# Paired heads in the neighbourhood attention, modulation's last third in the second block, and filter spectra from even and odd taps

## The reference

```python
# first block
s = einsum('bhqd,bhkd->bhqk', q, k) + c_i[..., :, None] - c[..., None, :]   # causal
x = layer_norm(alpha * x + concat(o_fox, o_hgrn) @ w_o)
x = layer_norm(alpha * x + (gelu(a) * u) @ w_down)          # a, u = split(conv(x @ w_up))
# second block
mod = silu(c) @ w_ada + b_ada                                # six vectors of 1024
sh1, sc1, g1, sh2, sc2, g2 = split(mod)
mod_c = silu(c_ctx) @ w_ada + b_ada
h = rmsnorm(x) * (1 + sc1) + sh1
s_nb  = einsum('brqhd,brikhd->bhrqik', rope(q), rope(k) in a window of 8x16) * scale + bias
s_ctx = einsum('brqhd,bchd->bhrqc', q, k_ctx) * scale        # 256 context tokens
p = softmax(concat(s_nb, s_ctx)); y_na = p @ concat(v, v_ctx)
K = rfft(concat(h_fwd, 0, h_bwd[:0:-1]), n=1024)             # filters, per order and channel
z = gate * irfft(rfft(z, n=1024) * K)                        # twice
x = x + g1 * gated_merge(...)                                # sh2, sc2, g2 modulate the FFN
```

## Time and profile before

| | us |
|---|---|
| median of 3 runs | 1770.71 (1770.68 to 1770.86) |
| the profiled execution | 1770.02 |
| its span, first to last instruction | 1768.2 |
| PE busy | 1663.8 (94%) |
| DVE busy | 891.2 (50%) |
| ACT busy | 657.0 (37%) |
| POOL busy | 267.3 (15%) |
| mean granted PE clock | 0.971 |

### The profile page before, as it was taken

The page is one execution under the profiler, slowest core; times in us unless marked ns, Lnnn a source line. Parts: engine busy times, 40 slices in busy tenths (PEclk is TensorE's granted clock), DMA queues, the critical chain, the costliest instruction groups (busy, mean ns, idle before and its releaser), DMA issues. The chain is left out here.

```text
span 1768.2 us, 19372 instructions
## 1 busy us (share of the span) xinstructions
PE 1663.8 (94%) x7952; PEld 1348.7 (76%) x7952; DVE 891.2 (50%) x1245; ACT 657.0 (37%) x888; POOL 267.3 (15%) x256
## 2 busy tenths in 40 slices
PE   5899989998998989999989999999799999999997
PEld 5668867767877868788788877777687888887885
DVE  6575446447787667633652543336864422223234
ACT  5544245443532233322542333333443522222222
POOL 0024302110511101100034011112432000000002
PEclk8999999999998989999999999999999999999998
DMA  7232222252244445422323322222444222222221
GB/s 276 96 131 84 72 83 91 82 197 96 84 178 167 191 167 191 145 94 95 110 90 109 119 100 87 82 75 90 175 147 167 95 93 90 89 91 92 96 72 48
DMA packets 47059, 204.86 MB, mean 116 GB/s; under 512 B 14353, under 2 KB 14737, under 8 KB 28219
## 3 DMA queue, kind: packets, MB, share of 16 engines
q1 hardware_dynamic: 37346, 172.89, 27.0%
q0 software_dynamic: 9088, 30.38, 4.9%
q10 hardware_dynamic: 536, 0.35, 0.1%
HBM read 182.60 MB, written 21.00 MB: 115 GB/s over the span
## 5 line engine op out<-in xcount | busy, mean ns | idle before, releaser
L438 PE MATMUL ps<-xh,whi 128*128 128x512 f32 (+1 forms) x1160 | 450.6, 388 | 16.4 <-DVE wlo L1563 10.4
L439 PE MATMUL ps<-xl,whi 128*128 128x512 f32 (+1 forms) x1160 | 445.0, 384 | 0.0
L440 PE MATMUL ps<-xh,wlo 128*128 128x512 f32 (+1 forms) x1160 | 442.6, 382 | 0.0
L1563 DVE TENSOR_TENSOR wlo<-raw,whi 128x2048 fp32r<-128x2048 f32 x114 | 273.7, 2401 | 277.3 <-ACT whi L1008 277.2
L1008 ACT ACTIVATE whi<-raw 128x2048 fp32r<-128x2048 f32 x114 | 217.2, 1906 | 186.8 <-PE ps L440 142.9
L438 PEld LDWEIGHTS ps<-xh,whi 128*128 128x128 f32 x1160 | 220.9, 190 | 80.6 <-issue 23.0
L440 PEld LDWEIGHTS ps<-xh,wlo 128*128 128x128 f32 x1160 | 220.4, 190 | 46.0
L439 PEld LDWEIGHTS ps<-xl,whi 128*128 128x128 f32 x1160 | 221.0, 190 | 42.3
L438 PE MATMUL ps<-whi,ah 128*128 128x512 f32 x352 | 139.7, 397 | 4.6 <-DVE al L1568 4.6
L439 PE MATMUL ps<-wlo,ah 128*128 128x512 f32 x352 | 139.5, 396 | 0.0
L440 PE MATMUL ps<-whi,al 128*128 128x512 f32 x352 | 139.5, 396 | 0.0
(11 more groups left out here) (383 smaller groups left out, 2660.6 us busy)
## 6 DMA issues: line engine op xcount, KB each, us to landing
raw<-in_w_in SPq DMA_DIRECT2D x35, 1024.0 KB, 4.9
raw<-in_ffn_w SPq DMA_DIRECT2D x33, 1024.0 KB, 4.8
raw<-in_ada SPq DMA_DIRECT2D x24, 1024.0 KB, 4.8
raw<-in_w_up SPq DMA_DIRECT2D x22, 1024.0 KB, 4.8
raw<-in_w_down SPq DMA_DIRECT2D x11, 1024.0 KB, 4.8
xd<-X POOLq DMA_DIRECT2D x8, 512.0 KB, 5.9
td<-vr POOLq DMA_DIRECT2D x16, 256.0 KB, 3.6
raw<-td SPq DMA_DIRECT2D x4, 1024.0 KB, 6.0
```

The lines of the kernel that those rows point to most:

```text
L438: pe.e.matmul(o, lh, rh, start=start, stop=False)
L439: pe.e.matmul(o, lh, rl, start=False, stop=False)
L440: return pe.e.matmul(o, ll, rh, start=False, stop=stop)
L1563: up(ve.e.tensor_tensor(lo, raw[conv_at[j] % 3][:, :], hi.bitcast(F32), ALU.subtract), "wlo")
```

## The change

Three parts, in one file.

- **Spectra.** Taps are ordered even first, then odd. One tile `dftf` holds cosines and sines for 256 frequencies. A part (`spectrum_part`) is one pair of even or odd taps' products: 32 parts of 3 matmuls where 32 halves had 6. ACT copies the even part to `spe`, the odd ones to `spo`. POOL adds and subtracts the two (16 operations on 128x512), which gives frequency f and frequency 512-f, waits for its own additions and starts the DMAs in pairs. The inverse tables of the later stage are reordered on the host.
- **Neighbourhood attention.** Items alternate between heads 2j and 2j+1. PE takes two banks every second iteration and issues four score products in a row: neighbourhood of the even head, of the odd one, context of the even head, of the odd one. POOL's biases come in the new order.
- **Modulation.** Group 2 (tiles 16 to 23) moves from FFN-up to the second block: DVE adds four tiles between the keys' and queries' rotations and four behind the conversions of the values' tiles; PE's call stands in the Hyena projection, in a row buffer of its own (`row3`). In FFN-up the tiles of groups 0 and 1 are spread over slots 1 to 19, and PE's calls stand behind slots 11 and 20; the context's channels behind slot 13. POOL's gate rows and three waits move with them.

```diff
-THIRDS = (8, 12, 20)
-def ada_beside(j):
-    return (j - 1,) if 1 <= j <= 8 else (2 * j - 10, 2 * j - 9) if 9 <= j <= 12 else (j + 3,) if 13 <= j <= 20 else ()
+ADA_UP = (1, 2, 3, 5, 6, 7, 9, 10, *range(12, 20))
+ADA_IN2 = (1, 2, 3, 4, 5, 5, 6, 6)
+def item(i):
+    return 2 * (i // 8) + i % 2, i % 8 // 2
+def bias_no(hd, v):
+    return 6 * (hd // 2) + 2 * v + hd % 2
...
-    several("dftf", 2)
+    several("dftf", 1)
...
-            def spectrum_half(n):
-                m = n // 2
-                i, f, hf = m // 4, m % 4, n % 2
-                th, tl = weights(J_DFT + i % 2)
+            def spectrum_part(n):
+                m, t = n // 2, n % 4
+                i, f = n // 8, n // 4 % 2
+                th, tl = weights(J_DFT)
                 h, l = weights(J_TAP + i)
...
-                for t in (2 * hf, 2 * hf + 1):
-                    x, c = 512 * t + P * f, slice(512 * t, 512 * t + 512)
-                    o = mm3(b[:, :], th[:, x:x + P], tl[:, x:x + P], h[:, c], l[:, c], t == 0, t == 3)
+                x, c = 1024 * (i % 2) + 256 * t + P * f, slice(512 * t, 512 * t + 512)
+                o = mm3(fills.bank["spec", m][:, :], th[:, x:x + P], tl[:, x:x + P], h[:, c], l[:, c], n % 2 == 0, n % 2 == 1)
...
-                    if 2 * j2 + part in THIRDS:
-                        ada(8 + 8 * THIRDS.index(2 * j2 + part))
-                if j2 == 5:
+                    if 2 * j2 + part in (11, 20):
+                        ada((11, 20).index(2 * j2 + part))
+                if j2 == 6:
...
                 used(J_H2 + c)
+                if c == 1:
+                    ada(2)
...
                 if i < 32:
-                    hd, t = divmod(i, 4)
-                    ht, po_ = hd // 2, 64 * (hd % 2)
-                    b = take(("as", 32 + i), "at_s", 32 + i + 1)
...
+                    if i % 2 == 0:
+                        ht, t = i // 8, item(i)[1]
+                        bs = [take(("as", 32 + i + o), "at_s", 32 + i + o + 1) for o in range(2)]
+                        for o, b in enumerate(bs):
+                            r = slice(64 * o, 64 * o + 64)
+                            keys = kr2[r, ht, :].rearrange("p (r c) -> p r c", c=64)[:, :, KC0[t]:KC0[t] + 32]
+                            pe.e.matmul(b[:, 0:256].rearrange("p (r c) -> p r c", c=32), qt[r, ht, P * t:P * t + P],
+                                        keys, start=True, stop=True)
+                        for o, b in enumerate(bs):
+                            r = slice(64 * o, 64 * o + 64)
+                            done(pe.e.matmul(b[:, 256:512], qn[r, ht, P * t:P * t + P], kc[r, ht, :],
+                                             start=True, stop=True), ("as", 32 + i + o))
                     gate_half(i)
...
-            high(J_DFT + 1)
...
-                ac.wait_ge(sig[f"kd{m % 3}"], 16 * (m // 3))
-                act(spk[m % 3][:, :], b[:, :], ACT.Copy, "sp_k", scale=2.0 / 1024)
+                u = m // 2
+                if m % 2:
+                    ac.wait_ge(sig[f"kd{u % 2}"], 32 * (u // 2))
+                    act(spo[u % 2][:, :], b[:, :], ACT.Copy, "sp_k")
+                else:
+                    ac.wait_ge(sig["kpm"], 2 * u)
+                    act(spe[:, :], b[:, :], ACT.Copy, "sp_k")
...
-            low_parts(J_DFT + 1)
+            low_parts(J_DFT)
...
                     low_parts(J_UP + 2 * j2 + part + 1)
-                    for n in (24,) if 2 * j2 + part == 21 else ada_beside(2 * j2 + part):
-                        ada(n)
+                    if 2 * j2 + part in ADA_UP:
+                        ada(ADA_UP.index(2 * j2 + part))
+                    if 2 * j2 + part in (12, 21):
+                        ada_sums((12, 21).index(2 * j2 + part))
...
                 up(ve.e.tensor_tensor(x[:, :], x[:, :], rope[:, 1, :], ALU.mult), "rt_m")
+                if n % 2:
+                    ada(16 + n // 2)
+            low_parts(J_V2 + 1)
+            ada(20)
+            ada(21)
             low_parts(J_V2 + 2)
+            ada(22)
+            ada(23)
...
                 low_parts(J_H2 + c + 1)
+                if c == 3:
+                    ada_sums(2)
...
+            ve.wait_ge(sig["gated"], 32)
...
-            def spectrum(m):
-                po.wait_ge(sig["sp_k"], m + 1)
-                po.e.dma_start(kd[m // 8, m % 8], spk[m % 3][:, :]).then_inc(sig[f"kd{m % 3}"], 16)
+            def spectrum(u):
+                i, f = u // 2, u % 2
+                a, b, s = spe[:, :], spo[u % 2][:, :], sps[u % 2][:, :]
+                po.wait_ge(sig["sp_k"], 2 * u + 2)
+                po.wait_ge(sig[f"kd{u % 2}"], 32 * (u // 2))
+                add(s, a, b, ALU.add, "kpm")
+                add(b, *((b, a) if i % 2 else (a, b)), ALU.subtract, "kpm")
+                po.wait_ge(sig["kpm"], 2 * u + 2)
+                po.e.dma_start(kd[i // 2, 4 * (i % 2) + f], s).then_inc(sig[f"kd{u % 2}"], 16)
+                po.e.dma_start(kd[i // 2, 4 * (i % 2) + 2 + f], b).then_inc(sig[f"kd{u % 2}"], 16)
...
-            spectrum(1)
             for k in range(4):
                 po.wait_ge(sig["hn_x"], k + 1)
                 c = slice(P * k, P * k + P)
                 add(orr[:, :, c], orr[:, :, c], gr[:, :, c], ALU.mult, "rec")
```

More of the change, by code:

```diff
@@ L90 @@
 rt_m hp hz mg_m gr_m f_a xa
-xg xb hd_p hx_p rec act rt_p rt_q zero bias hsum mg_a gr_x
-raw0 raw1 raw2 x0 x1d x2 x3 xsp consts mlp_in taps_in tri rows brow ncb0 ncb1 kd0 kd1 kd2 td0 td1 td2 td3 lvm ncd gated ctx tables
+xg xb kpm hd_p hx_p rec act rt_p rt_q zero bias hsum mg_a gr_x
+raw0 raw1 raw2 x0 x1d x2 x3 xsp consts mlp_in taps_in tri rows brow ncb0 ncb1 kd0 kd1 td0 td1 td2 td3 lvm ncd gated ctx tables
 tb0 tb1 tb2 tb3 rel0 rel1 vt kk0 kk1 kk2 tq0 tq1 tq2 tq3 tq4 tq5 tq6 hdl0 hdl1 hdl2 hdl3 put
@@ L157, in weight_plan @@
         plan.append(("w", ins["w_up"][i]))
-        for n in ada_beside(i - 1):
-            plan.append(("ada", ins["ada"][n]))
+        if i - 1 in ADA_UP:
+            plan.append(("ada", ins["ada"][ADA_UP.index(i - 1)]))
     several("w_down", 11)
-    several("w_in2", 20)
+    for i in range(20):
+        plan.append(("w", ins["w_in2"][i]))
+        for k, at in enumerate(ADA_IN2):
+            if i == at:
+                plan.append(("ada", ins["ada"][16 + k]))
     several("dfts", 2)
@@ L312, in build @@
         mx = [sb("mx", [P, S], F32, fs) for _ in range(2)]
-        spk = [sb("spk", [P, S], F32, fs) for _ in range(3)]
+        spe = sb("spe", [P, S], F32, fs)
+        spo, sps = ([sb(n, [P, S], F32, fs) for _ in range(2)] for n in ("spo", "sps"))
         fs.close()
@@ L870, in tensor_program @@
                 if i >= 3:
-                    hd, t = divmod(i - 3, 4)
+                    hd, t = item(i - 3)
                     c = slice(P * (hd // 2), P * (hd // 2) + P)
@@ L1301, in one @@
                     if inst == 0 and k == 3:
-                        ac.wait_ge(sig["gated"], 32)
+                        ac.wait_ge(sig["gated"], 16)
                     if k >= 4:
@@ L1416, in gate_rows @@
                 act(tm[k % 4][:, :], b[:, :], ACT.Copy, "sg")
+            tile(("adr", 2, 1))
             for i in range(34):
@@ L1712, in ada_sums @@
                 ve.wait_ge(sig["brow"], 16 * g)
+                r = row2 if g == 1 else row3
                 for h in range(2):
@@ L2351, in gpsimd_program @@
                 fox_bias(hd)
-                spectrum(2 * hd - 4)
-                spectrum(2 * hd - 3)
-            for m in range(12, 16):
-                spectrum(m)
+                spectrum(hd - 2)
+            spectrum(6)
+            spectrum(7)
             po.wait_ge(sig["pe"], at["w", J_TAP + 3])
@@ L2375, in gpsimd_program @@
                     gate_bias(0)
[L2376 to L2380 removed]
+            gate_rows(0)
+            po.wait_ge(sig["pe"], at["adr", 1, 1])
             po.e.dma_start(bcg[:, :], rows_of(ins["rows"], 4)).then_inc(sig["rows"], 16)
@@ L2428, in gpsimd_program @@
                 po.e.memset(x[:, 256:512], 0.0).then_inc(sig["zero"], 1)
-            for v in range(3):
-                bias(0, v)
-            for hd in range(8):
-                if hd < 7:
-                    bias(hd + 1, 0)
-                gate_out(2 * hd)
-                if hd < 7:
-                    bias(hd + 1, 1)
-                    bias(hd + 1, 2)
-                gate_out(2 * hd + 1)
+            for k in range(3):
+                bias(k)
+            for k in range(16):
+                n = 6 * (k // 4) + (3, 5, 6, 8)[k % 4]
+                for x in (n, n + 1) if k % 2 == 0 else (n,):
+                    if x < 24:
+                        bias(x)
+                gate_out(k)
             for n in range(2):
@@ L2537, in sync_program @@
             sp.wait_ge(sig["pe"], at["w", J_WO + 1])
-            for r, n in enumerate((6, 5, 5)):
-                sp.wait_ge(sig[f"kd{r}"], 16 * n)
+            for r in range(2):
+                sp.wait_ge(sig[f"kd{r}"], 128)
```

93 lines of the change are left out of this document (42 added, 51 removed).

## The result

The changed kernel takes 1726.6 us (median of 4 runs, 1725.28 to 1730.4) where the kernel before takes 1770.78 (4 runs). The ratio is 0.9754, with a 95% interval of 0.9737 to 0.9771: faster by 44 us, 41 to 47. The profiled execution took 1725.4 us with a span of 1723.6.

A forecast was written before the change was run, and what follows sets the result against it. The prediction took PE, busy 94% of the span, as the bound. Spectra 18.3, heads in pairs 16.7 and modulation 13.7 sum to 48.7 us; 1770.0 - 48.7 + 0.7 = 1722.0 us, range 1709 to 1733, to 1742 with rivals except the slow one.

The forecast's parts named there:

- The step ahead of the attention: Before the Fox attention: less ACT copying shortens a PE wait by 1.7 us and slow clock by 1.5, together 3.2.
- The failed term: Fox attention: 22.4 us of matmuls removed, of which 15.1 us would remain as gain after allowances for waits and POOL.
- the place at items 9 to 11: Fox loop: PE overtakes the softmax where DVE has an extra low part queued; 1.25 us subtracted.
- the rival "slower": Fox loop: small PE waits each iteration lower its clock, making the kernel slower, at worst about 1802 us; chance 0.025.
- the rival "filler hidden": Fox loop: softmax chain latency sets the pace, so parts 4 to 27 yield some 3 us; 1732 us, chance 0.11.
- two halves: Fox attention, POOL's additions: 1.0 us for delaying gating products and transposes, 1.0 us for slowing DVE's work.
- The four changes of 0.1 us: Neighbourhood attention: switching between kinds of matmul costs 0.4 us an iteration; pairing saves 0.4 a pair, 6.4 us in all.
- five slots: Neighbourhood attention: eight score passes, started in order on different rows, overlap into five slots, saving 10.3 us.
- two banks are taken at once, hence nothing: Neighbourhood attention: PE takes two banks an iteration earlier, but all have an iteration's slack; no cost.
- The first rival: Neighbourhood attention: the two heads' passes don't overlap, only fewer matmul changes gain, 6.4 rather than 16.7 us; 1732 us, chance 0.31.
- All three waits: FFN-up: PE waits of 1.64, 3.80 and 5.83 us go as modulation is spread thinner and calls stand later; 11.3 us.
- The cost at the queries: Second block: a modulation operation delays the queries' low part by 3.4 us, plus 0.9 for half clock; 4.3 us lost.

The follow-up runs named there:

- 9.9 alone: The kernel before with only the hunks of the spectra part: 1761.39 us, ratio 0.9944.
- 19.5 alone: The kernel before with only the hunks of the neighbourhood attention part: 1752.54 us, ratio 0.9890.
- on the same rows: The kernel before, with PE issuing the four score products of two successive items of one head in a row, all on the same 64 rows: 1765.86 us, ratio 0.9968.
- head by head: The changed kernel with a pair's score products reordered: neighbourhood and context of the even head, then of the odd one: 1727.76 us, ratio 0.9752.
- 20.4 alone: The kernel before with only the hunks of the modulation part: 1751.23 us, ratio 0.9885.
- mended: The changed kernel with DVE making the low part of the queries' first tile before adding modulation tile 16, later pairs likewise: 1727.01 us, ratio 0.9747.

## Why the prediction was right, and where it wasn't

The forecast was 1722.0, the result 1726.6, and the range held it. That the total came so near is in part luck. Alone, the spectra brought 8.4 us less than forecast and the two other parts 2.8 and 6.7 more, which nearly cancels; together the parts brought some 6 us less than their sum, of which the forecast knew nothing.

**Spectra: 18.3 forecast, 9.9 alone.** The step ahead of the attention was right: 3.2 forecast, and from the recurrence's earlier wait to its last one (at 225.59 and 266.09 when alone, at 225.05 and 268.76 before) the part gains 43.71 - 40.50 = 3.2; in the changed kernel (224.31 to 266.07) it is 1.9, with a clock of 0.50 rather than 0.63 over the 4 us behind the earlier wait. In the attention the sum took 22.4 down to 15.1; it was 5.3, and 3.4 alone. The failed term can be split by the two rows of the windows view. PE's idle time rose by 14.5 - 4.4 = 10.1 us, where the sum allowed 7.3: the start (2.5 us of waits for 2.3) and POOL's delay (1.24 for 1.0) came as sized, the end cost 2.7 for 1.8, and the place at items 9 to 11 was put at 1.25 and cost 3.0. The step read one late product off the trace (the low part beside it is the third tap tile's, at item 11, not one of w_o at item 9) but missed that ACT's queue holds a rounding that waits for DVE between two copies, so that DVE's low part reaches the softmax twice, in its own queue and in ACT's.

The other 6.9 us are PE's busy time: 113.78 - 22.4 = 91.4 us of work took 98.3, at a clock of 0.95. The sum had no term for this. From the rows above, 4.34 busy us at 0.63 and 6.82 at 0.52 cost some 4.9 of the 6.9 (an estimate); the other 2 are not traced, and the stretch behind 378.89 lies outside the window. It was the mechanism of the rival "slower" at a smaller size: the clock fell behind single waits, not through the loop, which kept 1.00 for 47 us with waits of 0.34 us in it. By its number the stage came out near the rival "filler hidden" (some 3 us from the loop), but not by its reason: where no extra work was queued an iteration took 2.76 us, and the longest wait went when one low part was moved.

**POOL's additions** were put at 2.0 us, in two halves. Their effect on waits was 3.0. On DVE's work it was worse than the 1.1 us an operation of the sum: an operation of 0.68 us took 3.6 beside POOL's products, which the additions had pushed into one burst (with the additions on 2 columns it took 2.33 at most).

```profile
292.59 3.62 DVE L1897 TENSOR_TENSOR vr<-vr,small 128x512 f32<-128x512 f32 x1
...
291.92 3.74 POOL L2299 TENSOR_TENSOR vr<-vr,gr 128x512 f32<-128x512 f32 x3
```

The DVE operation started in the first of POOL's three and ended 0.6 us after the third. The Trainium skill's page "SBUF — State Buffer", section "SBUF: two separate sides", says that these two engines share a pair of ports that one holds for a whole instruction while the other is blocked. These two rows agree with it as far as they go; why DVE lost to three operations in turn, no run here shows. The 2.28 us that became 2.92 show less, since an addition lasts 1.3.

**Heads in pairs: 16.7 forecast, 19.5 alone.** The four changes of 0.1 us were right: 6.4 forecast, 5.8 measured on the same rows. Overlap was expected and came, but whole: four slots for eight passes, 1.26 us a pair, 20.2 us, which is the estimate that the forecast made beside its own by the Trainium skill's page "TensorE: Matmul & The Clock Gate", section "Part 3: Packing small matmuls — row/col tiling". The trace decides for it here. The forecast's five slots came from passes that start in the program's order, as that page says of matmuls. The records of both orders (the changed kernel's, and head by head) show otherwise, and they decide. The step "two banks are taken at once, hence nothing" failed. That was one of the forecast's own signs of being wrong. It looked at the steady state, where each bank has an iteration's slack, and not at the first pair, whose second bank comes from the stage before: 2.5 us of wait and, in the changed kernel's profile, 1.6 of clock. DVE's wait for the gate rows shows as 4.0 us rather than 1, and was hidden as said. The first rival (no overlap, 1732) is out.

**Modulation: 13.7 forecast, 20.4 alone.** All three waits went (11.3), as said. Group 1's call gained 3.4, as said. The 64 sums gained 13.6 - 8.7 = 4.9 for 3.3. The rest of the 23.5 us that the stage gained, 3.9 us, is large matmuls that ran at half speed behind calls and waits; the sum left it out. Some 1.7 of it (an estimate) came by chance: it stood behind the wait of 2.20 us that the change left in place, where the clock over 4 us was 0.58 before (497.03) and 1.00 now (490.27). The cost at the queries was put at 4.3, of which 3.3 were seen to go when it was mended: 2.27 of wait and the clock. Why 2.27 and not 3.4: the operation ahead of the low part took 2.31 us, the lower bound.

So one error was made in both directions: waits of PE in FFN-up and in the Fox attention were priced by their length alone. Taking them away brought more, making them cost more, because of what the clock did behind them. At the first scores the wait itself was missing from the sum.

Of the other signs, PE's busy time in the Fox attention fell by 15.5 us rather than 22, and its mean iteration over items 3 to 31 was 3.24 us (3.39 before), just under the 3.3 that would have refuted the forecast; the wait at the queries was 2.27 for 3.4; FFN-up kept two waits over 1 us.

What stays open is where the slow clock falls in a given execution. The length of a wait doesn't settle it. The views of PE over the 4 us behind a wait of 3.13 us at the end of FFN-up, before and changed, and behind one of 2.66 us in the Fox attention before:

```profile
744.83:748.83 4.00, 4.00 (x17) 1.00 0.44 97
711.02:715.02 4.00, 4.00 (x11) 0.57 0.19 76
375.79:379.79 4.00, 3.98 (x28) 1.00 0.02 4
```

Likewise seven profiles have the wait of 2.53 us at the first scores with pairs on different rows; from there to the attention's end they take 154.1 to 154.2 us in four and 152.5 in three. Two profiles of the changed program had 112.82 and 116.31 us for the same Fox attention with the same waits in it, at a clock of 0.95 and 0.91.

## What to carry to other kernels

Price a new wait of the busiest engine by its length and, as the upper bound, by a slow stretch behind it (1 to 3.3 us here, when it came), and place it in its queue: who stands behind the instruction that waits, on the other engines too. When filler is taken from a loop, look at the one iteration that carries extra work, not at the mean; moving that work by three items took the longest wait away, at no cost in work. When an engine starts to take two buffers at once, look at the first time it does, where the second one still belongs to the stage before.

## What the hardware showed that was not expected

- Two float32 products on rows 0 to 63 and 64 to 127, into different banks, ran fully side by side: their passes start 0.007 us apart in the records, and 0.013 apart when the program has two products of one head ahead of the other's first. Eight passes took 1.07 us, on the same rows 1.93.
- The clock fell while PE did the 64 one-column matmuls, though no idle time stands ahead of them at 579.97: the first 32 took 3.5 us at 1.00, and the next 32 5.2 at 0.67. With the modulation alone the same happens at 586.59 (3.5 at 1.00, then 0.59). Rows alone say this; no run varied it.
- An operation of DVE beside three of POOL's took 3.62 us instead of 0.68.
